# An encoder kernel on Trainium2: the attention's output projection moved behind the attention units and done in three rounded passes

## Chip, cores, metric

The kernel runs on one core of a Trainium2 chip. The metric is the device time of one execution in microseconds (us); the number quoted for a kernel is the median of its runs.

## What is computed

Two encoder layers work on 544 tokens: 512 rows of a prompt (4 tiles of 128) and 32 sample rows (tile 4). Layer 0 has a pooling mixer, layer 1 an attention with 16 heads of 64; both are followed by a mixture of 32 experts of which each token takes two. The part that matters here:

```python
o = band_attention(q, k, v, ...)           # softmax(q k^T / 8 + bias) v, per head, 64-row chunks
y = jnp.einsum('bse,ed->bsd', o, w_o)      # output projection, (rows x 1024) x (1024 x 1024)
x = x + y
h = rms_norm(x, norm_ffn[1])
x = x + hier_moe(h, ...)                   # router, then silu(h w_gate) * (h w_up) @ w_down per expert
```

The projection is float32. The kernel may compute it with float32 matmuls, or with operands split in a rounded part and a rest: `hi*hi + lo*hi + hi*lo` (`split_product`, used in both kernels for the QKV product).

## The kernel before, in words

Each engine has its own program; semaphores join them. TensorE (PE) does the matmuls, VectorE (DVE) and ScalarE (ACT) work on their results, SyncE (SP) issues nearly all loads of weights in a fixed order, GpSimd (POOL) loads the attention's biases and gathers token rows.

**Attention of layer 1.** The work is 36 units: 32 of the prompt (`unit(t)`: tile 3 first, then 2, 1, 0, with 8 pairs of heads each) and 4 of the sample rows. A unit of tile i has i + 1 blocks of 128 keys, so units 0 to 7 have four key blocks, 8 to 15 three, 16 to 23 two, 24 to 31 one. An iteration t of the loop holds, on PE, the scores of unit t (L2353), the transposes of unit t-2 (L2377) and the product with the values of unit t-3 (L2393; samples L2407, L2409). Between them DVE adds the bias (L1770), ACT takes the exponential (L1253), DVE scales (L1782), and the transposed weights go from PSUM to SBUF by ACT for the first head (L1264) and by DVE for the second (L1790). After every fourth unit ACT copies the four pairs' outputs into `oT` (L1277, `oT_out`). Each engine keeps its own program order, so an operation put between two others delays what stands behind it.

**Output projection.** `products_at(t)` puts 16 portions of four float32 matmuls (L2443, `tile_product`) behind the values of an iteration: every second iteration from t = 12 to t = 34, and then t = 35 to 38 for tile 0. A float32 matmul is two MATMUL instructions in the trace. Two portions make half a tile; DVE adds it to `x` (`add_product`, L1798). ACT then takes the squares of a row tile for the norm (`early_squares`, L1289), DVE scales the rows (L1349), and ACT stores them to `xn` in DRAM (`store_row`, L993), from where the experts' rows are gathered. The sample rows' product (`sample_product`, L2421) stacks four k-blocks in the four column strips of the array; ACT copies the result (`wo_stack_out`, L1283) and `sample_fold` (L2428) adds the four. `w_o` is loaded in 8 pieces of 512 KB into the buffers `pair`, which are gate 1 and up 1 of the experts.

**Loads.** Experts' gate, up and down weights (2 MB each) have three buffers each. Loads of the first experts of layer 1 are issued during the attention where their buffer is free: down 1, gate 0, down 2. Up 0 and down 0 follow once the attention's last output is copied, gate 1 and up 1 once the projection is done (`att_y`), gate 2 when the router's second logits are done, up 2 when all rows are stored and the first block gathered. Those for expert 3 wait for the products of expert 0, quarter by quarter (L665), and so on.

**Routing.** After the projection: transposes of `x` (L1864), logits (L1930, L1940), a long chain on DVE, then the first block's gather and the experts.

## Time and profile before

| | us |
|---|---|
| median of 3 runs | 1343.85 |
| lowest and highest | 1343.29, 1345.46 |
| span of the profiled execution, first to last instruction | 1340.0 |
| PE busy in it | 1291.8 |
| VectorE, ScalarE, GpSimd busy in it | 574.1, 304.7, 127.9 |
| mean granted TensorE clock | 0.986 of full speed |

The profile gives the profiled execution by its span; the median of the runs, which also holds what lies around the span, is 3.85 us above it. TensorE's busy time is modelled for overlapping matmuls, so where a sum needs the pace of matmuls it is taken from the distance between their starts.

### The profile page before, as it was taken

How to read it: one execution, taken by the hardware profiler on the slowest of the kernel's cores; microseconds unless marked ns; L12 is line 12 of the kernel's file. 1: busy time of each engine (PE TensorE's matmuls, PEld its weight loads, DVE VectorE, ACT ScalarE, POOL GpSimd, SP SyncE). 2: the span in 40 equal slices, each digit the busy share in tenths (PEclk: the TensorE clock that was granted, in tenths of full speed). 3: DMA queues.
4: the chain of work that ended last, by engine and by line, in shares of the span. 5: the costliest groups of instructions: out<-in, count | busy, mean ns of one | idle time of the engine just before them, and what ended most of it. 6: DMA issues, size and time to landing. Idle time of an engine off the chain costs nothing.

```text
span 1340.0 us, 19743 instructions
## 1 busy us (share of the span) xinstructions
PE 1291.8 (96%) x7448; PEld 638.2 (48%) x7448; DVE 574.1 (43%) x1062; ACT 304.7 (23%) x650; POOL 127.9 (10%) x205
## 2 busy tenths in 40 slices
PE   8899999999999999999999999899999999999998
PEld 6643344333343334788777544443444334343333
DVE  4543334433333433864419543543334334343433
ACT  4211111111111113443436432211111111111111
POOL 2010000000000000232233210000000000000000
PEclk9989999999999999999999999899999999999999
DMA  9989999999999999222058512999999999999996
GB/s 360 380 334 420 424 428 426 427 429 427 428 427 427 428 425 402 69 93 97 34 174 273 181 33 78 380 344 420 426 427 426 427 428 428 427 428 427 426 426 255
DMA packets 53569, 459.65 MB, mean 343 GB/s; under 512 B 8141, under 2 KB 9421, under 8 KB 28170
## 3 DMA queue, kind: packets, MB, share of 16 engines
q1 hardware_dynamic: 41246, 426.48, 76.5%
q0 software_dynamic: 9616, 23.95, 5.5%
q10 hardware_dynamic: 2652, 8.45, 1.7%
q8 instruction: 39, 0.64, 0.2%
q14 instruction: 16, 0.13, 0.0%
HBM read 455.44 MB, written 11.26 MB: 348 GB/s over the span
## 4 chain that ended last, share of the span: by engine, by line
PE 91%; issue 3%; DVE 3%; ACT 2%; DMA 1%; POOL 0%; SPq 0%; DVEq 0%; ACTq 0%; POOLq 0%
PE ps L2014 34%; PE ps L2045 11%; PE ps L2023 9%; PE ps L2024 8%; PE ps L2443 4%; PE ps L1843 3%; PE ps L1845 3%; PE ps L1844 3%; PE ps L2006 2%; PE ps L2377 1%; PE ps L2393 1%; PE ps L1916 1%; PE ps L2032 1%; PE ps L2353 1%; PE ps L1864 1%
## 5 line engine op out<-in xcount | busy, mean ns | idle before, releaser
L1592 DVE TENSOR_TENSOR x<-x,ps 128x1024 f32<-128x1024 f32 (+1 forms) x150 | 177.7, 1216 | 220.9 <-PE ps L2045 219.8
L1606 DVE SCALAR_TENSOR_TENSOR nat<-nat,slot_gate,ps 64x256 f32<-64x256 f32 x128 | 86.1, 672 | 196.3 <-ACT nat L1093 164.7
L2014 PE MATMUL ps<-pair,xT 128*64 128x512 f32 x352 | 163.8, 616 | 6.1 <-issue 6.1
L2014 PE MATMUL ps<-ring,xT 128*64 128x512 f32 x352 | 160.9, 606 | 8.0 <-issue 6.4
L2015 PE MATMUL ps<-pair,xT 128*64 128x512 f32 x352 | 164.0, 616 | 0.0
L2045 PE MATMUL ps<-y_parts,hot 64*128 64x512 f32 (+1 forms) x1200 | 161.3, 403 | 0.0
L2015 PE MATMUL ps<-ring,xT 128*64 128x512 f32 x352 | 161.1, 607 | 0.0
L2014 PE MATMUL ps<-third_pair,xT 128*64 128x512 f32 x320 | 143.6, 596 | 6.9 <-issue 6.9
L1093 ACT ACTIVATE nat<-ps 64x512 f32<-64x512 f32 x62 | 36.8, 594 | 485.5 <-PE ps L2015 485.5
L2024 PE MATMUL ps<-qk,hidT 128*64 128x512 f32 x320 | 144.9, 595 | 0.0
L2023 PE MATMUL ps<-qk,hidT 128*64 128x512 f32 x320 | 144.8, 595 | 0.0
L2015 PE MATMUL ps<-third_pair,xT 128*64 128x512 f32 x320 | 143.8, 597 | 0.0
L2045 PEld LDWEIGHTS ps<-y_parts,hot 64*128 64x128 f32 (+1 forms) x1200 | 98.9, 171 | 72.3 <-issue 48.7
L1569 DVE TENSOR_TENSOR y_parts<-ps,y_parts 128x512 fp32r<-128x512 f32 x60 | 41.5, 692 | 132.5 <-ACT y_parts L1078 132.5
L2014 PEld LDWEIGHTS ps<-pair,xT 128*64 128x64 f32 x352 | 46.9, 140 | 97.2 <-issue 96.0
L2014 PEld LDWEIGHTS ps<-ring,xT 128*64 128x64 f32 x352 | 46.3, 139 | 96.5 <-issue 95.5
L2014 PEld LDWEIGHTS ps<-third_pair,xT 128*64 128x64 f32 x320 | 41.4, 137 | 85.8 <-issue 84.7
L2023 PE MATMUL ps<-ring,hidT 128*64 128x512 f32 x176 | 79.6, 595 | 1.6 <-ACT xT L1059 1.6
L2024 PE MATMUL ps<-ring,hidT 128*64 128x512 f32 x176 | 79.7, 596 | 0.0
L1078 ACT ACTIVATE y_parts<-ps 128x512 fp32r<-128x512 f32 x60 | 35.8, 597 | 192.4 <-PE ps L2024 192.4
L1843 PE MATMUL ps<-w_hi,hT_hi 128*128 128x512 f32 x192 | 76.8, 400 | 0.7 <-DVE hT_lo L1374 0.7
L769 POOL DMA_INDIRECT nat<-xn,gcol x30 | 30.7, 1022 | 467.9 <-PE ps L2006 428.8
(261 smaller groups left out, 1780.3 us busy)
## 6 DMA issues: line engine op xcount, KB each, us to landing
qk<-in_moe_w_down SPq DMA_DIRECT2D x40, 2048.0 KB, 28.5
ring<-in_moe_w_down SPq DMA_DIRECT2D x22, 2048.0 KB
ring<-in_moe_w_gate SPq DMA_DIRECT2D x20, 2048.0 KB, 23.7
ring<-in_moe_w_up SPq DMA_DIRECT2D x20, 2048.0 KB
third_pair<-in_moe_w_gate SPq DMA_DIRECT2D x20, 2048.0 KB, 22.7
third_pair<-in_moe_w_up SPq DMA_DIRECT2D x20, 2048.0 KB
pair<-in_moe_w_gate SPq DMA_DIRECT2D x18, 2048.0 KB
pair<-in_moe_w_up SPq DMA_DIRECT2D x18, 2048.0 KB, 29.7
```

The lines of the kernel that those rows point to most:

```text
L1569: V.tensor_tensor(y_rest[v], ps[:, bank, :], f32(y_high[v]), ALU.subtract).then_inc(y_lo[l], 1)
L1592: return V.tensor_tensor(x[0:n, i, :], x[0:n, i, :], ps[0:n, bank:bank + 2, :].rearrange("p b c -> p (b c)"), ALU.add)
L1606: last = V.scalar_tensor_tensor(out=out[u * BLK:(u + 1) * BLK, :].rearrange("s (k p) -> s k p", k=n), in0=act_rows[:, u * n:(u + 1) * n, : ...
L1843: mm(out, x_hi, w_h, start=start, stop=False)
L1844: mm(out, x_lo, w_h, start=False, stop=False)
L1845: return mm(out, x_hi, w_l, start=False, stop=stop)
L2014: mm(ps[BLK:P, GU_BANK, :], rows, gate[:, at], start=(k == 0), stop=(k == KT - 1))
L2015: last = mm(ps[0:BLK, GU_BANK, :], rows, up[:, at], start=(k == 0), stop=(k == KT - 1))
L2023: mm(ps[0:BLK, bank, :], rows, slot[:, at:at + 512], start=(k == 0), stop=(k == FT - 1))
L2024: last = mm(ps[BLK:P, bank, :], rows, slot[:, at + 512:at + D], start=(k == 0), stop=(k == FT - 1))
L2045: last = mm(ps[0:n, bank + hf, :], (hot[v] if by is None else by)[slots, tok(i)], part[slots, :], start=first and at == 0, stop=final and ...
L2443: last = mm(ps[:, WO_BANK, :], oT[:, k, tok(i)], wo_all[:, k, hf * 512:(hf + 1) * 512], start=(k == 0), stop=(k == KT - 1))
```

## The change

The projection leaves the units. Iterations 0 to 39 hold only attention. The attention's outputs are copied to `oT_raw`, then rounded by ACT into `oT_hi` (`oT_rounded`), and DVE writes the rest into `oT_lo` (`oT_rest`), once for every four units. `w_o` comes in 16 pieces of 256 KB (piece c is half `c // 8`, k-block `c % 8`); ACT rounds each (`wo_rounded`) and DVE takes its rest (`wo_rest`). Pieces 0 to 3 are loaded and split among the units (t = 28 to 32); the others are loaded once the last unit's values are done (`o_ps`), the last four into places that the first half has used. Behind the units PE runs 16 pieces for 4 tiles in three passes, 192 matmuls of 128x512, and 32 more for the sample rows, whose two parts stand side by side in 64 columns instead of four k-blocks in four strips. Every half tile has a PSUM bank of its own.

From unit 16 on, ACT copies the transposed weights of both heads in one instruction, and DVE none. Gate 1 and up 1, whose buffers no longer hold `w_o`, are loaded at the start of the attention. Gate 0, whose buffer now holds pieces, comes in two parts: three quarters behind the first use of the pieces and the last quarter after the last tile's product. `early_squares` of tiles 3 to 1 come behind all pieces; their row scaling moves into the routing, before the logits' operations on DVE, and their stores behind the logits on ACT. The transposes of `x` wait for the norms of tiles 3 to 1.

```diff
+        WO_QUAD, WO_PARTS = 4, 2 * KT
+        wo_parts = [nc.alloc_sbuf_tensor_at("wo_ring", [P, 4, 2, 512], F32R, offset=ring_at),
+                    nc.alloc_sbuf_tensor_at("wo_nat", [P, NT, 2, 512], F32R, offset=nat_at),
+                    nc.alloc_sbuf_tensor_at("wo_gain", [P, 1, 2, 512], F32R, offset=gain_at),
+                    nc.alloc_sbuf_tensor_at("wo_xT", [P, 1, 2, 512], F32R, offset=xT_at)]
+        WO_PLACES = [(0, 0), (0, 1), (0, 2), (0, 3), (1, 0), (1, 1), (1, 2), (1, 3), (1, 4), (2, 0), (3, 0)]
+        WO_PLACE = list(range(11)) + [3, 4, 5, 6, 7]
...
+        WO_BANKS = ((5, 3, 1, 7), (7, 4, 2, 0))
+        WO_SAMPLE_BANKS = (6, 5)
...
+        WO_SPLIT = 28
+        WO_LOADS = [(0, range(0, 4)), (1, range(4, 8)), (2, range(8, 11)), (0, range(11, 12)), (1, range(12, 16))]
...
+        def group_at(t, behind):
+            g, at = divmod(t - behind, OT_GROUP)
+            return g if at == 0 and 0 <= g < GROUPS_OUT else None
...
+            def load_wo(c):
+                hf, k = divmod(c, KT)
+                sp.dma_start(wo_raw(c), wo[:, k, hf * 512:(hf + 1) * 512]).then_inc(piece_in[wo_landed(c)[0]], 16)
+            GATE_FIRST = 3 * QUART
             for l in range(L):
                 if l == 1:
+                    sp.wait_ge(s_ps, 2)
+                    load_gate(1, 1, 1)
+                    sp.wait_ge(s_ps, PAIRS)
+                    load_up(1, 1, 1)
                     sp.wait_ge(s_ps, LONG_UNITS)
                     load_down(1, 1, 1)
                     sp.wait_ge(pT_ps, 2 * LONG_UNITS)
-                    load_gate(1, 0, 0)
+                    for c in range(WO_QUAD):
+                        load_wo(c)
                     sp.wait_ge(s_ps, PROMPT_UNITS)
                     load_down(1, 2, 2)
-                    sp.wait_ge(oT_sb, OT_ALL)
+                    sp.wait_ge(v_out, 16 * NT)
+                    sp.wait_ge(v_second_out, 16 * NT)
+                    sp.wait_ge(o_ps, UNITS)
+                    for c in range(WO_QUAD, KT):
+                        load_wo(c)
+                    load_up(1, 0, 0)
+                    for c in range(KT, KT + 3):
+                        load_wo(c)
+                    load_down(1, 0, 0)
+                    sp.wait_ge(quarters_used, QKV_QUARTERS + 1)
+                    load_wo(KT + 3)
+                    sp.dma_start(gate_slots[0][:, 0:GATE_FIRST], weights(wg, NEXP)[:, 0:GATE_FIRST]).then_inc(parts_in, 16)
+                    sp.wait_ge(quarters_used, QKV_QUARTERS + 2)
+                    for c in range(KT + WO_QUAD, WO_PARTS):
+                        load_wo(c)
+                    sp.wait_ge(att_y, 2 * TILES)
+                    sp.dma_start(gate_slots[0][:, GATE_FIRST:], weights(wg, NEXP)[:, GATE_FIRST:]).then_inc(gate_in[0], 16)
                 else:
                     load_gate(0, 0, 0)
-                load_up(l, 0, 0)
-                load_down(l, 0, 0)
-                if l == 0:
+                    load_up(l, 0, 0)
+                    load_down(l, 0, 0)
                     load_gate(l, 1, 1)
                     load_up(l, 1, 1)
                     sp.wait_ge(x_mixed[0], NT)
                     load_down(l, 1, 1)
                     load_down(l, 2, 2)
-                else:
-                    sp.wait_ge(att_y, 2 * NT)
-                    load_gate(l, 1, 1)
-                    load_up(l, 1, 1)
...
+            def oT_rounded(g):
+                act.wait_ge(oT_sb, 2 * g + 1)
+                if g == GROUPS_OUT:
+                    act.activation(oT_sample[:, :, 0, :], oT_sample_raw, ACT.Copy).then_inc(oT_sb, 1)
+                else:
+                    at, cols = oT_columns(g)
+                    act.activation(oT_hi[:, at, cols], oT_raw[:, at, cols], ACT.Copy).then_inc(oT_sb, 1)
+            def wo_rounded(c):
+                s, count = wo_landed(c)
+                act.wait_ge(piece_in[s], count)
+                act.activation(wo_part(c, 1), wo_raw(c), ACT.Copy).then_inc(split_hi, 1)
...
             for t in range(UNITS + 4):
-                if t >= 4 and t - 4 < PROMPT_UNITS and (t - 4) % OT_GROUP == OT_GROUP - 1:
-                    oT_out(t - 4)
+                if group_at(t, OT_GROUP + 3) is not None:
+                    oT_out(group_at(t, OT_GROUP + 3))
                 if t < UNITS:
                     weights(t)
                 if t == FFN_GAIN_FREE:
                     act.dma_start(ffn_gain[:, :], A["norm_ffn"][1:2, :].broadcast_to((P, D))).then_inc(ffn_gain_in, 16)
                 if 0 <= t - 2 < UNITS:
                     pT_out(t - 2)
-                for i, hf in halves_before(t - 1):
-                    if hf == 1 and i > 0:
-                        early_squares(i)
+                if group_at(t, OT_GROUP + 4) is not None:
+                    oT_rounded(group_at(t, OT_GROUP + 4))
+                if 0 <= t - WO_SPLIT < WO_QUAD:
+                    wo_rounded(t - WO_SPLIT)
                 if t == UNITS:
                     load_sqrt_table()
-                    act.wait_ge(act_own, own[0])
-                    act.activation(std[:, 3, 1:TILES], ssq[:, 3, 1:TILES], ACT.Sqrt, bias=const("eps"),
-                                   scale=1.0 / D).then_inc(std_ready, TILES - 1)
-            oT_out(UNITS - 1)
+            oT_out(GROUPS_OUT)
+            oT_rounded(GROUPS_OUT)
+            for c in range(WO_QUAD, WO_PARTS):
+                wo_rounded(c)
             for i in range(TILES - 1, 0, -1):
-                store_row(1, i)
+                early_squares(i)
+            act.wait_ge(act_own, own[0])
+            act.activation(std[:, 3, 1:TILES], ssq[:, 3, 1:TILES], ACT.Sqrt, bias=const("eps"),
+                           scale=1.0 / D).then_inc(std_ready, TILES - 1)
...
+            for i in range(TILES - 1, 1, -1):
+                store_row(1, i)
             logitsT_out(1, 1)
+            store_row(1, 1)
...
+                    if l == 1:
+                        for i in ((TILES - 1, TILES - 2), (TILES - 3,))[part]:
+                            scaled_rows(3, i, route_row(i), ffn_gain)
...
+            def wo_rest(c):
+                dve.wait_ge(split_hi, QKV_QUARTERS + c + 1)
+                V.tensor_tensor(wo_part(c, 0), wo_raw(c), f32(wo_part(c, 1)),
+                                ALU.subtract).then_inc(split_lo, 1)
             for t in range(UNITS + 4):
-                for i, hf in halves_before(t):
-                    add_product(i, hf)
                 if t < UNITS:
                     biased(t)
                 if 0 <= t - 1 < UNITS:
                     scaled(t - 1)
-                if 0 <= t - 2 < PROMPT_UNITS:
+                if 0 <= t - 2 < LONG_UNITS:
                     pT_out(t - 2)
-                if t == UNITS + 1:
-                    dve.wait_ge(std_ready, 3 * NT + TILES - 1)
-                    dve.wait_ge(ffn_gain_in, 32)
-                    link(V.reciprocal(rstd[:, 3, 1:TILES], std[:, 3, 1:TILES]))
-                if t > UNITS:
-                    i = TILES - 1 - (t - UNITS - 1)
-                    scaled_rows(3, i, route_row(i), ffn_gain)
+                if group_at(t, OT_GROUP + 5) is not None:
+                    oT_rest(group_at(t, OT_GROUP + 5))
+                if 0 <= t - WO_SPLIT - 1 < WO_QUAD:
+                    wo_rest(t - WO_SPLIT - 1)
+            oT_rest(GROUPS_OUT)
+            for c in range(WO_QUAD, KT + WO_QUAD):
+                wo_rest(c)
+            for i in range(TILES - 1, -1, -1):
+                add_product(i, 0)
+            for c in range(KT + WO_QUAD, WO_PARTS):
+                wo_rest(c)
+            for i in range(TILES - 1, -1, -1):
+                add_product(i, 1)
+            dve.wait_ge(std_ready, 3 * NT + TILES - 1)
+            dve.wait_ge(ffn_gain_in, 32)
+            link(V.reciprocal(rstd[:, 3, 1:TILES], std[:, 3, 1:TILES]))
...
+            def part_product(hf, i, k):
+                c = hf * KT + k
+                pe.wait_ge(split_lo, QKV_QUARTERS + c + 1)
+                return split_product(ps[:, WO_BANKS[hf][i], :], oT_hi[:, k, tok(i)], oT_lo[:, k, tok(i)],
+                                     wo_part(c, 1), wo_part(c, 0), k == 0, k == KT - 1)
+            def sample_product(hf, k):
+                c = hf * KT + k
+                pe.wait_ge(split_lo, QKV_QUARTERS + c + 1)
+                out = ps[:, WO_SAMPLE_BANKS[hf], :]
+                both = oT_sample[:, k, :, :].rearrange("p u t -> p (u t)")
+                if k == 0:
+                    mm(out[0:2 * SS, :], both, wo_part(c, 1), start=True, stop=False)
+                    return mm(out[0:SS, :], oT_sample[:, k, 0, :], wo_part(c, 0), start=False, stop=False)
+                mm(out[0:SS, :], oT_sample[:, k, 0, :], wo_part(c, 0), start=False, stop=False)
+                return mm(out[0:2 * SS, :], both, wo_part(c, 1), start=False, stop=(k == KT - 1))
...
             pe.wait_ge(kcT_sb, 2)
             for t in range(UNITS + 4):
                 if t < UNITS:
                     scores(t)
                 if t in (1, 2):
-                    keep_busy(1, WO_BANK, ident, some)
+                    keep_busy(1, SPARE_WO_BANK, ident, some)
                 if 0 <= t - 2 < UNITS:
                     p_transposes(t - 2)
                 if 0 <= t - 3 < UNITS:
                     values(t - 3)
-                if products_at(t) is not None:
-                    tile_product(*products_at(t))
+            pe.wait_ge(oT_lo_sb, GROUPS_OUT * (TILES - 1) // TILES)
+            for k in range(WO_QUAD):
+                for i in range(TILES - 1, 0, -1):
+                    part_product(0, i, k)
+            pe.wait_ge(oT_lo_sb, GROUPS_OUT)
+            for k in range(WO_QUAD):
+                part_product(0, 0, k)
+            pe.wait_ge(oT_lo_sb, GROUPS_OUT + 1)
+            for k in range(WO_QUAD):
+                last = sample_product(0, k)
+            last.then_inc(quarters_used, 1)
+            for k in range(WO_QUAD, KT):
+                for i in range(TILES - 1, -1, -1):
+                    last = part_product(0, i, k)
+                    if k == KT - 1:
+                        last.then_inc(att_y, 1)
+                last = sample_product(0, k)
+            last.then_inc(quarters_used, 1)
+            for k in range(KT):
+                for i in (TILES - 1, TILES - 2):
+                    last = part_product(1, i, k)
+                    if k == KT - 1:
+                        last.then_inc(att_y, 1)
+            for i in range(TILES - 3, -1, -1):
+                if i == 0:
+                    pe.wait_ge(x_half, TILES)
+                    for k in range(KT):
+                        last = sample_product(1, k)
+                    last.then_inc(stack_ps, 1)
+                for k in range(KT):
+                    last = part_product(1, i, k)
+                last.then_inc(att_y, 1)
+            pe.wait_ge(std_ready, 3 * NT + TILES - 1)
             transposes(3, TILES - 1)
-            for hf in range(2):
-                sample_product(hf)
```

TensorE, among the units with one key block (L2353 and L2468 scores, L2377 and L2492 transposes, L2393 and L2508 values, L2443 a portion of the projection). Before:

```order
L2353 MATMUL ps<-qk 128x128 x2
L2377 MATMUL ps<-cst,ring 128x128 x2
L2393 MATMUL ps<-ring,nat 64x128 x2
L2353 MATMUL ps<-qk 128x128 x2
L2377 MATMUL ps<-cst,ring 128x128 x2
L2393 MATMUL ps<-ring,nat 64x128 x2
L2443 MATMUL ps<-pair,third_pair 128x512 x4
L2353 MATMUL ps<-qk 128x128 x2
L2377 MATMUL ps<-cst,gain 128x128 x2
L2393 MATMUL ps<-ring,nat 64x128 x2
```

Now:

```order
L2468 MATMUL ps<-qk 128x128 x2
L2492 MATMUL ps<-cst,ring 128x128 x2
L2508 MATMUL ps<-ring,nat 64x128 x2
L2468 MATMUL ps<-qk 128x128 x2
L2492 MATMUL ps<-cst,ring 128x128 x2
L2508 MATMUL ps<-ring,nat 64x128 x2
L2468 MATMUL ps<-qk 128x128 x2
L2492 MATMUL ps<-cst,gain 128x128 x2
L2508 MATMUL ps<-ring,nat 64x128 x2
```

The portion behind every second iteration is gone; the attention's instructions are the same.

TensorE, at the end of the last units (L2407, L2409, L2522, L2524 values of the samples; L1864 the transposes of `x`). Before:

```order
L2409 MATMUL ps<-ring,nat 64x32 x2
L2443 MATMUL ps<-pair,third_pair 128x512 x4
L2407 MATMUL ps<-ring 64x32 x2
L2409 MATMUL ps<-ring,nat 64x32 x2
L2407 MATMUL ps<-ring 64x32 x2
L2409 MATMUL ps<-ring,nat 64x32 x2
L2443 MATMUL ps<-pair,third_pair 128x512 x4
L1864 MATMUL ps<-cst,x 128x128 x8
L2421 MATMUL ps<-pair,third_pair 32x512 x16
L1864 MATMUL ps<-cst,x 128x128 x8
```

Now (L1956 to L1958 are the three passes of `split_product`):

```order
L2524 MATMUL ps<-ring,nat 64x32 x2
L2522 MATMUL ps<-ring 64x32 x2
L2524 MATMUL ps<-ring,nat 64x32 x2
L2522 MATMUL ps<-ring 64x32 x2
L2524 MATMUL ps<-ring,nat 64x32 x2
L2522 MATMUL ps<-ring 64x32 x2
L2524 MATMUL ps<-ring,nat 64x32 x2
L1956 MATMUL ps<-wo_ring,oT_hi 128x512
L1957 MATMUL ps<-wo_ring,oT_lo 128x512
L1958 MATMUL ps<-wo_ring,oT_hi 128x512
L1956 MATMUL ps<-wo_ring,oT_hi 128x512
```

What stood between the samples' values is now one run of 224 matmuls behind them, and the transposes of `x` follow that run.

ScalarE, units 29 to 31 (L1253 and L1307 exponentials, L1264 and L1321 copies of transposed weights, L1277 and L1337 copies of outputs, L1353 the rounding of a piece). Before:

```order
L1264 ACTIVATE ring<-ps 128x128
L1253 ACTIVATE ring<-ring 128x128 x2
L1264 ACTIVATE ring<-ps 128x128
L1277 ACTIVATE third_pair<-ps 128x4x128
L1253 ACTIVATE gain,ring<-gain,ring 128x128 x2
L1264 ACTIVATE ring<-ps 128x128
L1253 ACTIVATE ring<-ring 128x160
```

Now:

```order
L1321 ACTIVATE ring<-ps 128x2x128
L1353 ACTIVATE wo_ring<-ring 128x512
L1307 ACTIVATE ring<-ring 128x128 x2
L1321 ACTIVATE ring<-ps 128x2x128
L1353 ACTIVATE wo_ring<-ring 128x512
L1337 ACTIVATE third_pair<-ps 128x4x128
L1307 ACTIVATE gain,ring<-gain,ring 128x128 x2
L1321 ACTIVATE ring<-ps 128x2x128
L1353 ACTIVATE wo_ring<-ring 128x512
```

A rounding of a piece stands behind each copy, and the copy takes both heads.

## Rows read from the trace of the kernel before

**Rows 1.** The page: span, and GB/s of the DMA engines in 40 slices of 33.5 us.

```profile
span 1340.0 us, 19743 instructions
...
GB/s 360 380 334 420 424 428 426 427 429 427 428 427 427 428 425 402 69 93 97 34 174 273 181 33 78 380 344 420 426 427 426 427 428 428 427 428 427 426 426 255
```

**Rows 2.** Window of 20 us: busy of PE, PEld, DVE, ACT, POOL; clock, DMA share, GB/s.

```profile
860.00:880.00 20.00, 17.82 (x65) 8.18 (x66) 17.26 (x63) 2.55 (x5) 1.98 (x2) 0.85 0.77 296
```

**Rows 3.** Timeline of SyncE's DMA queue: start, length, line, target and source.

```profile
858.63 0.33 SPq L617 DMA_DIRECT2D third_pair<-in_moe_w_gate  x1
...
877.02 0.33 SPq L665 DMA_DIRECT2D ring<-in_moe_w_gate  x1
```

**Rows 4.** Chain that ended last: start, length, engine, tile, line.

```profile
731.41 0.85 PE ps L2353 x8
...
736.53 3.63 PE ps L2443 x8
...
822.51 3.63 PE ps L2443 x8
...
827.30 3.63 PE ps L2443 x8
...
840.30 0.89 PE ps L1864 x8
```

**Rows 5.** Instruction groups, 704 to 841 us: shapes, count, busy us, mean ns.

```profile
L2443 PE MATMUL ps<-pair,third_pair 128*128 128x512 f32 x128 | 59.2, 605 | 0.0
...
L1277 ACT ACTIVATE third_pair<-ps 128x512 f32<-128x512 f32 x8 | 4.6, 579 | 0.0
```

**Rows 6.** Timeline of a one-key-tile unit: start, length, engine, line.

```profile
801.69 0.49 PE L2353 MATMUL ps<-qk 64*128 64x128 f32 x4
...
802.66 0.40 ACT L1253 ACTIVATE ring<-ring 128x128 f32<-128x128 f32 x1 [3.14 <-DVE ring L1770]
...
803.44 0.25 ACT L1264 ACTIVATE ring<-ps 128x128 f32<-128x128 f32 x1
...
803.75 0.44 PE L2377 MATMUL ps<-cst,ring 128*128 128x128 f32 x2 [0.41 <-ACT ring L1264]
...
804.49 0.70 PE L2443 MATMUL ps<-pair,third_pair 128*128 128x512 f32 x1
```

**Rows 7.** Timeline of a two-key-tile unit.

```profile
757.64 0.70 PE L2353 MATMUL ps<-qk 64*128 64x256 f32 x4
...
758.95 0.51 ACT L1253 ACTIVATE ring<-ring 128x256 f32<-128x256 f32 x1 [4.79 <-DVE ring L1770]
...
760.58 0.63 PE L2377 MATMUL ps<-cst,ring 128*128 128x128 f32 x4
```

**Rows 8.** DVE group in the QKV product, 543 to 700 us.

```profile
L1361 DVE TENSOR_TENSOR w_lo<-ring,w_hi 128x1024 fp32r<-128x1024 f32 x20 | 31.0, 1563 | 46.3 <-ACT w_hi L940 46.2
```

**Rows 9.** Timeline of ScalarE among the last units.

```profile
827.87 1.28 ACT L960 ACT_TABLE_LOAD   x1
```

**Rows 10.** Timeline of TensorE in the QKV product.

```profile
542.82 0.39 PE L1843 MATMUL ps<-w_hi,hT_hi 128*128 128x512 f32 x1
...
545.77 0.39 PE L1844 MATMUL ps<-w_hi,hT_lo 128*128 128x512 f32 x1
```

**Rows 11.** Timeline of TensorE and ScalarE behind the last tile product.

```profile
841.17 3.64 PE L2421 MATMUL ps<-pair,third_pair 128*32 128x512 f32 x32
...
844.49 1.06 ACT L1283 ACTIVATE gain<-ps 128x512 f32<-128x512 f32 x2
...
847.66 1.50 PE L1864 MATMUL ps<-cst,x 128*128 128x128 f32 x11
```

**Rows 12.** DMA issues, 690 to 900 us: count, KB each, median us to landing.

```profile
xn<-third_pair ACTq DMA_DIRECT2D x4, 512.0 KB, 10.8
...
ring<-in_rel_bias_reversed POOLq DMA_DIRECT2D x5, 256.0 KB, 6.1
```

**Rows 13.** Window of 1 us in the routing; columns as in the second group.

```profile
856.00:857.00 1.00, 1.00 (x8) 0.87 (x9) 0.54 (x2) 0.00 (x0) 0.00 (x0) 0.50 0.96 410
```

150 lines of the change are left out of this document (76 added, 74 removed).

## The prediction

> **What bounds the kernel now.** I read the page first, then the windows of the routing, SyncE's queue, the chain of waits, and last the timelines of single units. The page's GB/s line has two plateaus near 427, one for each layer's experts, and a valley between them, the attention [rows 1]. Two facts follow. Once the second plateau is reached the experts are paced by their weights, so whatever the change gains or loses before it shifts the end by as much. And the plateau doesn't begin when a weight happens to be ready early: in the routing the DMA engines already have slack, 0.77 busy over 20 us [rows 2], and expert 3's first quarter is issued only at 877.02, when expert 0 has used its buffer [rows 3]. Before expert 0 starts, all free buffers are full in both kernels. So gate 1 and up 1 during the attention save nothing by themselves: they only restore what moving `w_o` out of their buffers and behind the units would otherwise delay.
>
> What is left is the path from iteration 12 of the units to the routing. In the chain it is nearly all TensorE: iterations and portions of the projection in turn, each portion 3.63 us, from the first at 736.53 to the transposes of `x` at 840.30 [rows 4], 103.8 us. The 64 float32 matmuls are 128 instructions in that stretch [rows 5]; 16 portions x 3.63 = 58.1 us. The other 45.7 us are iterations 13 to 39. They are so short because each portion hides the latency of a unit: the other engines finish their step while TensorE multiplies.
>
> **Term 1, the units without portions: +7.1 us.** I rebuild iterations 13 to 39.
> - Three key blocks: 731.41 to 736.53 is two iterations without a portion, 2.56 each [rows 4]. Three of them (13 to 15) take 7.7. Iterations 16 to 18 mix three and two blocks; at about 2.35 they take 7.1.
> - Two key blocks: the loop goes through two iterations. Scores' start to exponential's start is 1.31, from there to the transposes 1.63, and the transposes and values take about 0.60 each [rows 7]: 4.14, with the larger copy of both heads 4.2, so 2.1 each. Five iterations: 10.5.
> - One key block: 801.69 to 804.49 is two iterations, 2.80 [rows 6]; the exponentials hold ScalarE 0.78 (802.66 to 803.44), the copy is now twice as long, so 1.45 to 1.5 each. Iterations 26 and 27: 3.0. Iterations 24 and 25, with two-block transposes, about 1.8 each: 3.6.
> - Iterations 28 to 32 carry the pieces. ScalarE has 0.78 + 0.35 + a rounding of 0.55 (priced as the copy of 512 columns, 0.579, less its overlap [rows 5]) = 1.7, and 2.3 where a group's copy or rounding joins. VectorE has two biases, the scaling and a subtraction of half the size of the one in the QKV product, 1.563 / 2 = 0.78 [rows 8], so also about 1.9 to 2.3. I take 2.3, 2.3, 1.8, 2.3, 1.6: 10.3.
> - Samples, 33 to 35: TensorE's own small matmuls, 1.5 + 1.4 + 2.0 = 4.9. Iterations 36 to 38: 827.30 - 822.51 - 3.63 = 1.16 each [rows 4], 3.5. The last copy stands behind a group's rounding (0.55) and the table load of 1.28 [rows 9], of which TensorE covers some 0.5: +1.3, so 4.8.
> - The copy of a group's output, which the next values wait for, was hidden by a portion; I give these waits 1.0.
>
> The sum is 7.7 + 7.1 + 10.5 + 3.0 + 3.6 + 10.3 + 4.9 + 4.8 + 1.0 = 52.9 against 45.7, rounded +7.1. Bounds: +1 if only TensorE's work counted, +13 if each wait is exposed in full.
>
> **Term 2, the portions go: -58.1 us**, as above.
>
> **Term 3, the run of rounded products: +50.8 us.** The QKV product has the same form of three passes; 542.82 to 545.77 is 13 intervals, 0.227 us each [rows 10]. 64 products x 3 = 192, and the samples' 32 (two for each of 16 pieces): 224 x 0.227 = 50.8. The samples alone cost 7.3, where four strips at once took 3.64 [rows 11]. Cover for the pieces: 4 to 7 are loaded when the last values end, while 56 matmuls (12.7 us) on pieces 0 to 3 run. The last four wait for the first half and are wanted 24 matmuls, 5.4 us, later. A 256 KB load that shares the engines with a 2 MB load takes 6.1 us [rows 12], with 0.6 + 0.8 for rounding and rest 7.5; that would expose 2.1. By then no other load is left in the queue, so I take 0 and keep +2.1 as the bound.
>
> **Term 4, behind the run: -1.9 us.** From the end of the last portion, 840.30, to the next pair of transposes at 847.66 were 7.4 us, of which the samples' product took 3.64 [rows 4, 11]. It has moved into term 3. But the fold still waits for ScalarE's stacked copies, which started at 844.49 behind the squares of tile 0 [rows 11]; these need the last product just as before. So only about half of 3.64 comes out; bounds 0 and -3.6.
>
> **Costs taken at nothing.** Row scaling of tiles 3 to 1 in the routing, 3 x about 1.2 us of VectorE, stands ahead of logits for which VectorE waited; if that cover were too small, up to 1 us. The stores of these rows: tile 1's is now issued just behind the load of gate 2, issued at 858.63 [rows 3]. A store under load took 10.8 us [rows 12], which ends near 870, when the first gather is about to start; 0, bound +3. Gate 1 and up 1 share the engines with the first biases, as the eight pieces of `w_o` did before: 0, bound +1.
>
> **Sum.** +7.1 - 58.1 + 50.8 - 1.9 = -2.1 us: the profiled span goes from 1340.0 to 1337.9, and the median, 3.85 above the span before, from 1343.85 to **1341.8**. Two kernels of this length can be told apart at about 0.2%, 2.7 us, so this is within what counts as no change, by little.
>
> **One rule against the change.** Where TensorE has short, sparse work, its granted clock is at the lower level, 0.50 of full speed (1.2 GHz) in the window at 856 [rows 13], and 0.85 on average over 860 to 880, that is 6 of 20 us at half [rows 2]. In the units it never fell, and each pair of them contained a portion of dense work. The Trainium skill (TensorE: Matmul & The Clock Gate, section "HAM oscillation") says that bursts of matmuls with idle time between them make the clock fall again each time, so that the next burst starts slow. By that rule the units with one key block, which now leave TensorE idle a quarter to a half of the time, would run at the lower level, and so would the first stretch of the product; the sum would be that of the first rival.
>
> **The rivals.**
> - *Slower: the clock falls in the short units.* At half speed the scores, transposes and values of one block (0.42 + 0.37 + 0.37 = 1.16 by the starts in [rows 6]) add 1.16 to two iterations, 0.58 each, to 15 iterations at most 8.7; with half of it hidden or at the full clock, 4.3. The product's first stretch at half clock, as long as the 6 us of [rows 2], costs 3. Together +7: 1349. For: iterations 28 to 35 are paced by the others. Against: TensorE is still busy over half of each iteration, and the clock stayed up among the three-block units without portions. It decides from +4.8 us on. Chance 0.22.
> - *Faster: the latencies hide after all.* If ScalarE and VectorE keep up, term 1 is +1.5 and the time is 1336.2. For: two iterations in [rows 6] took 2.80 including a wait of 0.41, so the loops are not far above TensorE's own work. Against: that pair started with everything ready. Chance 0.16.
> - *Faster: bytes.* If the end is set by bytes alone, 4 MB loaded earlier at 427 GB/s are 9.8 us: 1332. Against: the buffers, as said. Chance 0.04.
> - *Late pieces or stores.* +3: 1345. Chance 0.10.
>
> **How the numbers follow.** My forecast has 0.48, with its own range 1338.5 to 1345. Below 1341.15 (faster) lie nearly half of it, 0.20, and both faster rivals: 0.40. Within 2.7 us of 1343.85 lie the rest of it and most of the late pieces: 0.35. Slower is the clock's case and a remainder: 0.25. The range 1335 to 1350 holds the two large rivals and leaves out the bytes and the far ends of the bounds.
>
> **What would show it.** Right: iterations of two blocks near 2.1 us and of one block near 1.5, about 2 with pieces; last values near 789; 224 matmuls in 50.8 us without a wait; transposes of `x` near 840; the first quarter of expert 3 some 2 us earlier than 877. A clock of 0.5 between 765 and 800 shows the first rival, a gap in the middle of the run late pieces, a first gather that waits for stores the late stores. The forecast is wrong if the last values end before 785 or after 794, or if expert 3's first quarter moves by another amount than the end of the kernel.

## The result, and the profile after

The changed kernel takes 1348.66 us, the median of 13 executions, beside 1343.29 us for the kernel before on the same chip. The ratio is 1.0037, with a 95% interval of 1.0028 to 1.0047: +5.0 us, slower by more than the 0.2% that can be told apart. Taken again later (e15 below) it was 1.0032 (1.0016 to 1.0048). The forecast of 1341.8 was wrong, and the time is that of the first rival, 1349; it lies within the range of 1335 to 1350.

The profiled execution took 1347.7 us with a span of 1345.9, so 1.8 us lie around the span. By the same 1.8 the profiled execution of the kernel before took 1341.8. Between the two spans are 5.9 us, of which 2.3 were there before anything changed: the first unit's scores start at 699.92 in the one and at 702.22 in the other. Over all profiled executions below, of kernels whose programs are equal up to there, this start lay between 698.0 and 707.5, so it differs from execution to execution. It goes with the clock as well. The changed kernel's profile has 6.8 us at half clock from 15.4 on, the one before has none there (the window from 14 to 24, first of the kernel before and then of the changed one; the clock is the third number from the end). In e13, the latest start, 10.2 us are at half clock from 14.4 on, and 3.4 each near 485 and 564:

```profile
14.00:24.00 10.00, 9.02 (x66) 8.51 (x66) 5.96 (x8) 5.13 (x10) 7.12 (x8) 1.00 1.05 382
14.00:24.00 10.00, 10.00 (x48) 9.02 (x47) 5.77 (x8) 5.13 (x10) 7.38 (x9) 0.66 1.04 389
```

What is left to explain in the profile is +3.6 us, against the -2.1 forecast: 5.7 us.

The page of the changed kernel, by the side of [rows 1]. The second plateau of GB/s begins in the slice in which it began before (the 28th, 419 and 420):

```profile
span 1345.9 us, 19904 instructions
...
PEclk8989999999999999999999979889999999999999
DMA  9889999999999999222057663489999999999996
GB/s 363 350 333 420 426 426 427 427 427 427 429 427 429 426 425 402 71 91 96 34 182 254 184 227 124 145 316 419 427 426 428 427 427 426 429 428 427 427 425 258
```

New in the clock's line are the 7, the slice from 774 to 807, and the 8 of the first slice, which has a 9 in the kernel before. Windows of the last units, the samples and the first product matmuls (start:end, length, busy of PE, PEld, DVE, ACT, POOL, clock, DMA share, GB/s):

```profile
770.00:774.00 4.00, 3.42 (x32) 1.95 (x28) 2.51 (x17) 3.66 (x15) 2.21 (x6) 1.00 0.39 74
774.00:778.00 4.00, 2.58 (x22) 1.40 (x20) 3.73 (x17) 3.86 (x14) 0.78 (x2) 1.00 0.61 136
778.00:782.00 4.00, 2.70 (x41) 1.72 (x42) 3.07 (x14) 3.54 (x12) 0.20 (x1) 0.74 0.98 296
782.00:786.00 4.00, 4.00 (x56) 2.47 (x48) 2.02 (x9) 2.11 (x8) 0.00 (x0) 0.50 0.65 270
...
794.00:798.00 4.00, 4.00 (x12) 3.14 (x12) 0.42 (x1) 0.58 (x2) 0.00 (x0) 0.62 0.72 231
798.00:802.00 4.00, 4.00 (x20) 3.28 (x19) 2.12 (x4) 2.19 (x4) 0.00 (x0) 1.00 1.06 424
```

TensorE is busy 2.58 and 2.70 of 4 us from 774 to 782, with ScalarE at 3.86 of 4 in the first of them, and its clock falls at 780.0 to 0.50 of full speed (1.2 GHz). It comes back at 797, in the run of products. From 782 on TensorE itself bounds the samples, busy 4.00 of 4. In the kernel before the clock was 1.00 over all of this stretch:

```profile
774.00:778.00 4.00, 3.57 (x30) 2.23 (x29) 3.60 (x16) 3.02 (x11) 1.64 (x3) 1.00 0.19 31
```

The timeline of TensorE at the start of the run shows the matmuls at both levels, 0.43 us from start to start and then 0.22 to 0.24:

```profile
793.66 0.80 PE L1956 MATMUL ps<-wo_ring,oT_hi 128*128 128x512 f32 x1
794.26 0.63 PE L1957 MATMUL ps<-wo_ring,oT_lo 128*128 128x512 f32 x1
794.68 0.63 PE L1958 MATMUL ps<-wo_ring,oT_hi 128*128 128x512 f32 x1
...
797.16 0.40 PE L1958 MATMUL ps<-wo_ring,oT_hi 128*128 128x512 f32 x1
797.40 0.39 PE L1956 MATMUL ps<-wo_ring,oT_hi 128*128 128x512 f32 x1
```

Ahead of all this, from 714 to 775, the chain of waits of the changed kernel goes twelve times through a load of a unit's bias, 3.35 to 10.17 us each; in the kernel before it does so once (3.54 us at 782.77). Two of the twelve:

```profile
768.27 3.35 DMA gain<-in_rel_bias_reversed
771.91 3.36 DMA ring<-in_rel_bias_reversed
```

In the middle of the run the last four pieces are late. They are issued at 821.12, rounded from 826.67, their rests follow from 827.33, and TensorE, whose matmul before them started at 826.17, goes on at 828.08, 1.7 us late:

```profile
821.12 1.75 SPq L664 DMA_DIRECT2D nat<-in_attn_w_o  x4
...
826.67 2.19 ACT L1353 ACTIVATE wo_nat<-nat 128x512 fp32r<-128x512 f32 x4 [12.33 <-DMA nat<-in_attn_w_o]
827.33 2.50 DVE L1904 TENSOR_TENSOR wo_nat<-nat,wo_nat 128x512 fp32r<-128x512 f32 x4 [5.97 <-ACT wo_nat L1353]
...
828.08 0.50 PE L1956 MATMUL ps<-wo_nat,oT_hi 128*128 128x512 f32 x1 [1.52 <-DVE wo_nat L1904]
```

Behind the run, the chain of waits of the changed kernel (start, length, engine, tile, line), the counterpart of [rows 4, 11]:

```profile
848.43 0.89 PE ps L1977 x8
...
881.02 0.61 PE ps L2127
```

From 848.43 to expert 0's first matmul at 881.02 are 32.6 us, where the kernel before took 34.75 (840.30 to 875.05). Expert 3's first quarter is issued at 882.99, 5.97 later than in [rows 3], and the end is 5.9 later: what happens ahead of the experts comes out at the end one for one.

### The profile page after: what moved, and what is told of

Its sections match the earlier page's. It is cut to its first block, busy times and chain, and to the rows that moved or that the text cites. A ratio compares the mean times of both kernels' runs of the same rounds, so it can differ in the third digit from the quotient of the medians.

```text
span 1345.9 us, 19904 instructions
## 1 busy us (share of the span) xinstructions
PE 1288.9 (96%) x7512; PEld 659.4 (49%) x7512; DVE 585.6 (44%) x1071; ACT 321.3 (24%) x675; POOL 128.3 (10%) x205
## 4 chain that ended last, share of the span: by engine, by line
PE 88%; DMA 5%; issue 3%; DVE 3%; ACT 2%; SPq 0%; POOL 0%; DVEq 0%; ACTq 0%; POOLq 0%
PE ps L2127 33%; PE ps L2158 11%; PE ps L2136 9%; PE ps L2137 8%; PE ps L1956 4%; PE ps L1958 4%; PE ps L1957 4%; DMA ring<-in_rel_bias_reversed 2%; PE ps L2119 2%; PE ps L2029 1%; PE ps L2145 1%; DMA ffn_gain<-in_rel_bias_reversed 1%; PE ps L2367 1%; PE ps L1977 1%; DMA gain<-in_rel_bias_reversed 1%
## 5 line engine op out<-in xcount | busy, mean ns | idle before, releaser
L2127 PE MATMUL ps<-pair,xT 128*64 128x512 f32 x352 | 160.8, 607 | 5.9 <-issue 5.9
L2128 PE MATMUL ps<-pair,xT 128*64 128x512 f32 x352 | 160.9, 607 | 0.0
L1956 PE MATMUL ps<-w_hi,hT_hi 128*128 128x512 f32 x192 | 76.8, 400 | 0.7 <-DVE hT_lo L1459 0.7
```

Source lines behind the costliest of these rows:

```text
L1956: mm(out, x_hi, w_h, start=start, stop=False)
L2127: mm(ps[BLK:P, GU_BANK, :], rows, gate[:, at], start=(k == 0), stop=(k == KT - 1))
L2128: last = mm(ps[0:BLK, GU_BANK, :], rows, up[:, at], start=(k == 0), stop=(k == KT - 1))
```

## The experiments

My theory was now the first rival's: the clock. Its rivals were the late pieces, the loads of gate 1 and up 1 among the units, and the stores and loads behind the run. Fifteen kernels went to the chip in four sets, and each set shares some 29 executions of the kernel before. "Ratio" is to the kernel before, with its 95% interval; the clock is TensorE's mean over each span, averaged over all executions of a kernel. The kernel before stands at 0.986 in each set. e4 and e8 have 6 executions, e9 has 7, the others 12 or 13. The clock in the last column is that of the whole span and does not say where in it the clock was low.

| kernel | median us | ratio | mean clock |
|---|---|---|---|
| the change | 1348.66 | 1.0037 (1.0028 to 1.0047) | 0.979 |
| e1 wide dummies | 1349.35 | 1.0038 (1.0021 to 1.0055) | 0.983 |
| e2 three tiles | 1346.61 | 1.0024 (1.0011 to 1.0036) | 0.979 |
| e3 33 matmuls among the samples | 1347.62 | 1.0031 (1.0015 to 1.0046) | 0.984 |
| e4 gate 1, up 1 behind the run | 1350.80 | 1.0053 (1.0033 to 1.0073) | 0.977 |
| e5 gate 2 behind the stores | 1346.35 | 1.0039 (1.0020 to 1.0057) | 0.979 |
| e6 18 early matmuls, three tiles | 1342.62 | 0.9994 (0.9981 to 1.0008) | 0.982 |
| e7 = e6 and e5 | 1340.68 | 0.9985 (0.9970 to 1.0000) | 0.983 |
| e8 gate 1, up 1 behind the stores | 1351.70 | 1.0063 (1.0041 to 1.0084) | 0.978 |
| e9 kernel before with e5's edit | 1347.64 | 1.0044 (1.0021 to 1.0066) | 0.984 |
| e10 = e7, 21 early, from step 26 | 1339.26 | 0.9986 (0.9969 to 1.0003) | 0.984 |
| e11 18 dummies, three tiles | 1346.47 | 1.0029 (1.0015 to 1.0044) | 0.982 |
| e12 = e7 again | 1342.02 | 0.9986 (0.9968 to 1.0004) | 0.983 |
| e13 one thin dummy a step, three tiles | 1344.26 | 1.0007 (0.9989 to 1.0025) | 0.982 |
| e14 two thin dummies a step | 1346.02 | 1.0011 (0.9996 to 1.0026) | 0.984 |
| e15 the change again | 1347.27 | 1.0032 (1.0016 to 1.0048) | 0.979 |

### e1: dummies of full width

```diff
+                if 24 <= t < UNITS:
+                    w = 512 if t < PROMPT_UNITS else 256
+                    mm(ps[:, SPARE_WO_BANK, 0:w], ident, some[:, 0:w], start=True, stop=True, skip_group_check=True)
```

> The changed kernel with one dummy matmul a unit behind the scores of units 24 to 35 on TensorE (128x512 f32, 0.59 us at the full clock, for units 24 to 31; half as wide for 32 to 35), into the bank that stands idle there; everything else as in the change. The changed kernel stands at 1.0037 of the kernel before (+5.0 us). Theory A (the granted clock of 0.50 between 780 and 797 costs the sample units and the first product matmuls their time): the clock stays at 1.00 through 770 to 800, the first seven product matmuls take 0.227 us each in place of about 0.43 (-1.6), the sample units come every 1.5 instead of 2.0 us (-2 to -3), the dummies lie in TensorE's waits; the kernel gets 3 to 4.5 us faster than the change, +0.5 to +2 against the kernel before. Rival B (the units are paced by ScalarE and VectorE or by the bias loads, and the clock only follows): the last values end where they did, 793.7, or later by what of the 12 dummies (6 us) isn't hidden; -1.6 at best, up to 3 us slower.

A miss by the time: 1.0038, the change's own. In its profile the clock held through the last units and most of the samples (it fell at about 791), but the dummies of 0.59 us pushed the units back: the scores of unit 24 start at 763.4 and the last prompt unit's at 779.0, 15.6 us later; in the change from 764.8 to 776.6, 11.8 us. In the profile, then, what the clock gave the samples was largely paid by the dummies, and the end of the clock's fall still hit the run (0.50 from 794 to 798). The experiment tells neither way.

### e2: three tiles on pieces 8 to 11

```diff
             for k in range(KT):
-                for i in (TILES - 1, TILES - 2):
+                for i in (TILES - 1, TILES - 2, TILES - 3) if k < WO_QUAD else (TILES - 1, TILES - 2):
                     last = part_product(1, i, k)
...
-                for k in range(KT):
+                for k in range(WO_QUAD if i == TILES - 3 else 0, KT):
                     last = part_product(1, i, k)
```

> The changed kernel with pieces 8 to 11 of the output weights multiplied for three tiles (3, 2, 1) before piece 12 is asked for, not for two: 36 rounded matmuls (8.2 us at 0.227) stand between the last use of pieces 4 to 7 and the first of piece 12, in place of 24 (5.4). Nothing else moves. Theory A (pieces 12 to 15 are late: loads issued at 821.12 land in 4.2 us, rounding and rest take until 828.08, TensorE stands about 1.9 us and the piece-paced start a little more): the gap closes wholly, 1.5 to 2.5 us faster than the change. Rival B (the time behind the run is set by the row scaling and the stores or by the first expert's weights, so that an earlier end of the run is given back): the run ends 2 us earlier, but the time is that of the change within 0.5 us.

The gap is gone from the trace, the run has no wait left, and the ratio falls from 1.0037 to 1.0024, about 1.7 us (the intervals overlap). That is theory A, and the size of the gap itself. The run still took 53.7 us, because in this execution the clock stayed at 0.50 until about 798.

### e3: 33 matmuls among the last units and samples

```diff
+            EARLY = {30: [(3, 0)], 31: [(3, 1)], 32: [(3, 2)], 33: [(3, 3)], 34: [(2, 0), (2, 1)],
+                     35: [(2, 2), (2, 3)], 36: [(1, 0)], 37: [(1, 1), (1, 2)], 38: [(1, 3)]}
...
                     values(t - 3)
+                for i, k in EARLY.get(t, ()):
+                    pe.wait_ge(oT_lo_sb, (TILES - i) * PAIRS // OT_GROUP)
+                    part_product(0, i, k)
-            for k in range(WO_QUAD):
-                for i in range(TILES - 1, 0, -1):
-                    part_product(0, i, k)
```

> The changed kernel with 33 of the 36 rounded matmuls of pieces 0 to 3 for tiles 3, 2 and 1 put among the last units and samples (three or six behind the values of each step, from unit 30 on) and not all behind them; the banks are those of the change. Theory A (TensorE has idle time in the short units and samples, and real matmuls there take work out of the run and keep the clock up): 33 times 0.227 = 7.5 us leave the run, the last values end 3 to 5 us later than at the full clock, about where they did at 793.7; the clock may still fall at 780, since the first of them comes at 777; 3 to 6 us faster than the change. Rival B (TensorE is the bound of the samples, at half clock 2.0 of 2.04 us a unit busy, so that a matmul put there only moves): the last values end 7.5 to 10 us later and the time is that of the change within 1 us.

The clock never fell from 766 to 806. 7.5 us of matmuls were added and the last values ended only 3.1 us later than in the change (796.8 for 793.7). But the ratio was only 0.0006 better, 0.8 us, and the profile shows both places where the gain went. First, pieces 4 to 7 can be loaded only when the last values have read `v_nat`, and now too little work covered them. In the timelines of TensorE and VectorE of this kernel:

```profile
805.34 0.50 PE L1956 MATMUL ps<-wo_nat,oT_hi 128*128 128x512 f32 x1 [3.06 <-DVE wo_nat L1904]
...
804.59 1.90 DVE L1904 TENSOR_TENSOR wo_nat<-nat,wo_nat 128x512 fp32r<-128x512 f32 x3 [6.43 <-ACT wo_nat L1353]
```

Second, the chain behind the run goes through the last row's store:

```profile
864.98 11.10 DMA xn<-third_pair
...
876.94 2.75 DMA nat<-xn,gcol_first
```

### e4: gate 1 and up 1 behind the products

```diff
-                    sp.wait_ge(s_ps, 2)
-                    load_gate(1, 1, 1)
-                    sp.wait_ge(s_ps, PAIRS)
-                    load_up(1, 1, 1)
...
+                    sp.wait_ge(att_y, 2 * NT)
+                    load_gate(1, 1, 1)
+                    load_up(1, 1, 1)
```

> The changed kernel with the loads of gate 1 and up 1 (2 MB each) taken out of the attention and put behind the products, where the kernel before has them. Theory A (these 4 MB hold back the bias loads of units 3 to 12, whose landing took 7.3 us once): the waits of GpSimd on the biases before unit 12 shrink, unit 12's scores start up to 1 us earlier; the time falls by 0 to 1 us. Rival B (they cost nothing there, and save bandwidth behind the run, where gate 2, up 2 and expert 0's quarters are loaded): the same within 0.5 us, or 0.5 to 2 us slower if the loads behind the run collide with the gathers and the first expert's weights.

Slower by 2 us, as the third part of rival B says, and its profile shows the price of the clock into the bargain. The units before 775 differ little: from the first scores to those of the last prompt unit are 73.9 us, and 74.3 in the change. So the loads in the attention cost the units 0.4 us, although GpSimd waited 7.4 us for one bias there. But from the last prompt unit's scores to the last values' end are 13.4 us (775.5 to 788.9) where the change took 17.2 (776.56 to 793.73): here the clock was 1.00 until 786.2, although TensorE was busy only 2.13 of 4 us from 774 to 778.

```profile
774.00:778.00 4.00, 2.13 (x20) 1.22 (x24) 3.93 (x18) 4.00 (x16) 0.40 (x2) 1.00 0.84 208
778.00:782.00 4.00, 3.64 (x67) 2.25 (x68) 3.53 (x16) 3.38 (x12) 0.00 (x0) 1.00 0.95 385
782.00:786.00 4.00, 3.81 (x62) 2.65 (x60) 1.65 (x8) 3.17 (x13) 0.00 (x0) 1.00 0.21 86
786.00:790.00 4.00, 3.58 (x33) 2.89 (x32) 0.43 (x2) 2.16 (x6) 0.00 (x0) 0.53 0.01 4
```

I read these 3.8 us as what the half clock costs the samples; it is the difference of one profile of each of two kernels. All of it is lost again behind the run, where 4 MB issued at 850.15 and gate 2 at 860.96 run beside the last store, 14.71 us in the chain:

```profile
861.65 14.71 DMA xn<-third_pair
```

### e5: gate 2 waits for the row stores

```diff
                 sp.wait_ge(logitsT_ps, 2 * (l + 1))
+                if l == 1:
+                    sp.wait_ge(xn_stored[l], 16 * NT)
                 load_gate(l, 2, 2)
```

> The changed kernel with one edit on the queue of loads: gate 2 of the second layer (2 MB, issued at 864.57 in the changed kernel, just as the last row store is issued) waits until the stores of the normalised rows have landed. Theory A (the rest of the loss behind the products is the stores sharing the DMA engines with gate 2: where the chain of waits goes through the last store it takes 11.1 us, in the run with gate 1 and up 1 there as well 14.7): the last store lands some 5 us earlier, the gather of the first expert's rows goes when VectorE's row numbers are there (about 874 on the changed kernel's clock, for 876.2), expert 0 starts 1 to 2 us earlier, the time falls by 1 to 2 us. Rival B (the row numbers of VectorE and GpSimd's own start set the gather, not the store): the same within 0.5 us, or slower by up to 1 if gate 2 comes late.

Not decided: the ratio is that of the change (1.0039), with a wide interval. In its profile expert 0 starts 31.4 us behind the run, where the change took 32.6. In the change's own profiled execution the first gather waited for VectorE's row numbers, not for a store; in the profile of the change taken again (e15) it did wait for the store, which was issued 0.7 us behind gate 2 and took 10.57 us. So the collision is there in some executions of the same kernel and not in others.

### e6 and e7: 18 early matmuls, and gate 2 behind the stores

```diff
+            EARLY = {30: [(3, 0)], 31: [(3, 1)], 33: [(3, 2)], 35: [(3, 3)], 37: [(2, 0)], 38: [(2, 1)]}
...
+                for i, k in EARLY.get(t, ()):
+                    pe.wait_ge(oT_lo_sb, (TILES - i) * PAIRS // OT_GROUP)
+                    part_product(0, i, k)
...
                 for i in range(TILES - 1, 0, -1):
-                    part_product(0, i, k)
+                    if (i, k) not in sum(EARLY.values(), []):
+                        part_product(0, i, k)
```

That is e6, with e2's edit; e7 has e5's as well.

> The changed kernel with 18 rounded matmuls (pieces 0 to 3 of tile 3, pieces 0 and 1 of tile 2) spread three by three over the steps 30, 31, 33, 35, 37, 38 of the units, and pieces 8 to 11 multiplied for three tiles before piece 12. 38 matmuls (8.8 us at 0.23) are left to cover the 8.5 us from the last values to piece 4, where the run with 33 early ones stood 3.1 us. Theory A (the loss is the clock that falls, 4 us in the samples and 1.6 to 1.9 in the first product matmuls, and the late pieces, 1.5 to 3): the clock stays at 1.00 through 800, no gap over 0.5 us in the run, the last values end 1.5 to 3 us before the changed kernel's (samples at full clock -4, early matmuls +1 to +2.5), the run takes 206 times 0.23 = 47.5 us; the products end 6 to 9 us earlier than in the change; with the start of the first expert following by three quarters or more, the time falls by 5 to 8 us, to 1 to 3 us below the kernel before. Rival B (what is gained at the products' end is given back behind it, to stores and loads, as in the run with 33 early ones, where 2 of 3.4 us were): the products end as said, but the time falls by 2 to 4 us.

> Both edits of the two kernels before this one in one: 18 matmuls among the last units and samples, three tiles on pieces 8 to 11, and gate 2 behind the row stores. Theory A (clock, late pieces and the collision of stores and gate 2 are three separate costs): its time is that of the kernel with 18 early matmuls less 2 us or more, since the more the products end early the more the store is the last; 7 to 10 us below the change, 2 to 5 below the kernel before. Rival B (the store isn't what is late): the same as with 18 early matmuls alone, within 0.7 us.

e6 is 4.0 us faster than e2 by medians and no longer to be told from the kernel before. Its profile keeps the clock at 1.00 through the samples and has no gap; the last values end 89.8 us behind the first scores (the change 91.5), the run from there takes 47.8 us (the change 54.6). Together that is 8.5 us. 1.7 of them are given back behind the run, where the chain now goes through a store of 10.60 us, so that 6.8 reach the end of the profile; by ratio it is 5.8 against the change. The mean clock, 0.977 to 0.986 over the executions, leaves room for a fall among the units in some of them. e7 takes another 1.9 us off by medians (1.2 by ratio, and the intervals overlap), with the chain now past the stores. These are windows of e7, to be set beside the change's:

```profile
774.00:778.00 4.00, 3.48 (x22) 2.09 (x22) 3.07 (x17) 3.32 (x12) 0.20 (x1) 1.00 0.93 215
778.00:782.00 4.00, 3.77 (x57) 2.27 (x59) 3.37 (x13) 3.05 (x11) 0.00 (x0) 1.00 0.93 385
...
794.00:798.00 4.00, 4.00 (x20) 3.25 (x18) 0.24 (x1) 0.91 (x2) 0.00 (x0) 1.00 0.93 336
```

### e8 and e9: the same wait elsewhere

```diff
                 sp.wait_ge(logitsT_ps, 2 * (l + 1))
+                if l == 1:
+                    sp.wait_ge(xn_stored[l], 16 * NT)
+                    load_gate(1, 1, 1)
+                    load_up(1, 1, 1)
                 load_gate(l, 2, 2)
```

This is e8, with e4's loads taken out of the attention. e9 is the kernel before with e5's two lines.

> The changed kernel with gate 1 and up 1 out of the attention, loaded behind the row stores and before gate 2, which waits for the stores too. The run with these two loads right behind the products was 2 us slower than the change: its products ended 4.2 us earlier (start of the units taken out), but the last store took 14.7 us. Theory A (the loads in the attention cost the units nothing, the 4 us were the clock, which fell 6 us later there by chance; the loss was the store): the units run as in the change, with the clock falling somewhere between 778 and 790, the last store takes 5 to 6 us, and the time is that of the run with stores first, within 1 us. Rival B (the 4 MB in the attention do hold the units up by 4 us): the last values end again at 789 to 790, and with the store free the time is 4 us or more below the change.

> The kernel before with the one edit of the stores: gate 2 of the second layer waits until the normalised rows have landed; nothing of the change. It tells what of the 2 us between the kernels with 18 early matmuls without and with this edit belongs to the change. Theory A (the collision of the last row store with gate 2 is in the kernel before as well, its stores took 10.8 us and it stood 34.75 us behind the products): 1 to 2.5 us faster than the kernel before. Rival B (in the kernel before the store isn't what ends last, since expert 0's weights and the rows leave the queue in another order): the same within 0.5 us; then the whole 2 us are won from the change's shape.

Both are misses on the time and agree with each other. e8's units run as e4's to 0.1 us, and its clock falls at 786.3, e4's at 786.2, where in the four profiles with these loads in the attention and no matmuls added (the change, e2, e5, e15) it falls at 772 to 780. So the later fall isn't mere chance of one execution, though what sets it stays open; and rival B's "4 us or more below" doesn't come, since the loads now meet the gather. In e8 it took 8.58 us and in e9 5.75, where it took 2.75 to 3.07 in the other chains that pass it. e8's chain:

```profile
872.51 8.58 DMA nat<-xn,gcol_first
```

and e9's:

```profile
871.91 5.75 DMA nat<-xn,gcol_first
```

Behind the stores comes the gather, and a 2 MB load put off from the one lands on the other. In the kernel before the chain doesn't pass the stores, though they took 10.8 us [rows 12], so there the wait only costs. In the profiles expert 0 starts 36.9 us behind the products for 34.9, and from there to the end another 1.3 us are lost: 3.3 of the 5.9 us that the ratio of 1.0044 makes. With 7 executions, the rest stays open. What e5's edit gains in e7 belongs to that kernel's order of things.

### e10 and e12: pieces rounded earlier, and e7 once more

```diff
-        WO_SPLIT = 28
+        WO_SPLIT = 24
...
+            EARLY = {26: [(3, 0)], 28: [(3, 1)], 29: [(3, 2)], 31: [(3, 3)], 33: [(2, 0)], 35: [(2, 1)], 37: [(2, 2)]}
```

> The kernel with 18 early matmuls and stores first, but pieces 0 to 3 are rounded four units earlier (from unit 24 on, not 28), and 21 matmuls stand among the units from step 26 on in place of 18 from step 30. 35 matmuls and more (8.1 us) are left for the 8.5 us to piece 4. Over all its executions the kernel with 18 had a mean clock of 0.983 (0.977 to 0.987), the kernel before 0.986, the change 0.979. Theory A (the clock still falls in some executions because TensorE idles before its first early matmul at about 775): the mean clock over the executions rises to 0.985 or more and the time falls by another 1 to 2 us. Rival B (TensorE is by no means idle in the two-block units, and ScalarE and VectorE bound the short ones, into which the roundings move): no more than 0.5 us either way, or 0.5 to 1.5 us slower, from the two-block units with 1.4 us more of rounding work.

> The kernel with 18 early matmuls, three tiles and stores first once more, on the chip of the other three, so that it stands beside them and beside the kernel before a second time. It stood at 0.9985 [0.997, 1.0000]. Theory A (its gain is real): 0.9975 to 0.9990 again, 7 us below the change. Rival B (the first set of executions was a lucky one for the clock): 0.9995 to 1.0010.

e7's gain repeats (0.9986), on another chip. e10 gives the same ratio, with a median 2.8 us lower than e12's and 3.9 below the kernel before, but with an upper interval that reaches 1.0003: rival B within what can be told. The clock rose only from 0.983 to 0.984.

e12's profile is worth more than its ratio. It is the same program as e7, both profiled executions start their units at 700.3, and up to unit 30 they agree to within 1 us (its scores start at 772.64 in e7 and at 772.20 in e12). Then e12's clock falls, from 774.6 to 781.4 and again from 791.6 to 798.4, where e7's stays at 1.00. e12:

```profile
774.00:778.00 4.00, 3.89 (x19) 2.12 (x17) 2.91 (x16) 2.87 (x11) 0.20 (x1) 0.57 0.74 182
778.00:782.00 4.00, 4.00 (x44) 2.47 (x42) 2.09 (x8) 2.05 (x8) 0.00 (x0) 0.58 0.89 332
...
794.00:798.00 4.00, 4.00 (x11) 3.13 (x10) 0.00 (x0) 0.00 (x0) 0.00 (x0) 0.50 1.01 341
```

Neither has a wait in its run. e12's run ends at 843.04 and e7's at 838.17, 4.9 us apart, and the spans are 1340.9 and 1336.4. So within one program 13.7 us at half clock in this stretch went with 4.9 us more. It also shows that 18 matmuls among the units don't hold the clock in every execution.
Three sets of executions of this shape stand about 1.9 us below the kernel before in ratio, each with an interval that just reaches 1; against the change, 6 to 7 us less by ratio, they are clear.

### e11, e13, e14: activity alone

e11 has the places of e6 but three dummies at each, and the whole run behind; e13 and e14 have one or two dummies where TensorE waits for ScalarE's copy. All have e2's edit; e13 and e14 also round pieces 0 to 3 from unit 24 on. This is e13; e14 has `range(2)`.

```diff
+                if t == 27:
+                    pe.wait_ge(split_lo, QKV_QUARTERS + 1)
+                    pe.wait_ge(oT_lo_sb, 1)
+                if 27 <= t < 40:
+                    for _ in range(1):
+                        mm(ps[:, SPARE_WO_BANK, :], oT_hi[:, 0, tok(TILES - 1)], wo_part(0, 1), start=True, stop=True)
```

> The kernel with three tiles on pieces 8 to 11, plus 18 rounded dummy matmuls at the places where the kernel with 18 early ones has real ones (steps 30, 31, 33, 35, 37, 38), of the same operands, into the idle bank; the run behind the units is whole, all 224 matmuls. So no work leaves the run, and only TensorE's activity among the units is added. The kernel with three tiles had a mean clock of 0.979 over its executions and stood at 1.0024 of the kernel before, the one with 18 real early matmuls 0.982 and 0.9994. Theory A (the clock is the larger part of the change's loss, 4 us in the samples and 1.9 behind them, and activity alone brings it back): the clock keeps up through the samples, the last values end 1.5 to 3 us before those of the kernel with three tiles, the run loses its 1.9 us of half clock: 3 to 4.5 us faster in an execution in which the clock holds, 1.5 to 3.5 us faster by medians. Rival B (the 4 us between those two kernels are the 18 matmuls that left the run, 4.1 us, and the clock is worth little): the same as the kernel with three tiles within 1 us, or up to 2 us slower from the 4.1 us of added matmuls.

> The kernel with three tiles on pieces 8 to 11, plus one rounded dummy matmul (128x512, 0.23 us) behind the scores of each step from 27 to 39, where TensorE waits some 0.6 us for ScalarE's copy; pieces 0 to 3 are rounded from unit 24 on. No matmul leaves the run. Theory A (the clock alone is worth 3 to 5 us where it holds): the clock at 780 to 790 stays at 1.00 in the profiled execution, the mean clock over the executions rises from 0.979 to 0.982 or more, 2 to 4 us faster than the change repeated beside it by medians beyond the 1.5 of the three tiles (so 3.5 to 5.5 in all). Rival B (the gain of the kernels with early matmuls is the work that left the run): 1 to 2 us faster than the change, that of the three tiles, whatever the clock. Rival C (a third of a microsecond a step is too little to hold it): the clock falls as before and the time is B's.

> The same with two dummy matmuls a step (26, 6.0 us in all, of which some 0.45 us a step in TensorE's waits). Theory A: the clock holds more surely than with one (mean over the executions 0.983 or more), and costs little where TensorE waits but up to 0.2 us a step in the samples: 2 to 5 us faster than the change. Rival B: the time of the three tiles or up to 2 us slower than that.

> The changed kernel as it is, beside the two with dummies. All theories: 1.0030 to 1.0045 of the kernel before, mean clock over the executions 0.978 to 0.980 where the kernel before has 0.986; in the profiled execution the clock falls somewhere between 774 and 790 and comes back at 796 to 800.

e11 held the clock in its profiled execution and was 3.4 us faster in it than e2 (span 1341.1 for 1344.5, with the first scores at 700.3 and 700.6), but not by medians: over its executions the clock was 0.979 to 0.986, and the 4.1 us of dummies are there in each of them. e13 and e14 put less in. With one thin dummy a step and no work taken out of the run, e13 is at 1.0007, where the change beside it is at 1.0032: 3.0 us by medians (1344.26 for 1347.27), of which 1.7 are e2's. So activity alone, less what the dummies cost, is worth 1 to 2 us by medians. Over e13's twelve, the four with a clock of 0.980 or less took 1346.9 to 1350.5 us, the eight above it 1341.8 to 1346.2. But this is the clock of the whole span: e13's profiled execution is one of the four, and of its 59.7 us at half clock only 10.2 lie near the samples (792.7 to 802.9), while 30.7 lie ahead of the units, whose scores start at 707.45, 5 us later than the change's. That is less than theory A's 2 to 4, and more than rival B's none; the difference of 1.3 us over B is at the edge of what the intervals bear. e14 is at 1.0011, 1.3 us below e15 by medians and 2.8 by ratio; below theory A's 2 to 5 by the one and within it by the other. It holds the clock in its profiled execution from 774 to the end of the run, but behind the run the chain goes through a store of 11.00 us and 4 us are lost against the change's profile:

```profile
782.00:786.00 4.00, 4.00 (x57) 2.59 (x55) 2.46 (x14) 2.90 (x11) 0.00 (x0) 1.00 0.70 295
786.00:790.00 4.00, 4.00 (x52) 2.94 (x48) 1.13 (x3) 2.58 (x6) 0.00 (x0) 1.00 0.01 2
790.00:794.00 4.00, 4.00 (x35) 3.06 (x36) 0.42 (x1) 1.32 (x5) 0.00 (x0) 1.00 0.17 45
```

Its run of 224 matmuls at the full clock without a gap took 51.1 us (792.52 to 843.59): 0.228 each. e15's profile shows the change itself with another pattern, the clock at 0.50 from 772.0 to 778.8 and from 785.7 to 792.5, earlier at both ends than I had expected, and the same wait of 1.5 us for the late pieces.

## Why the prediction was wrong

**By its own steps.** In the profile the terms came out so:

| step | predicted | measured |
|---|---|---|
| start of the units | 0 | +2.3, from execution to execution |
| term 1, units without portions | +7.1 | +9.2 |
| term 2, the portions | -58.1 | -58.1 |
| term 3, the run | +50.8 | +54.7 |
| term 4, behind the run | -1.9 | -2.2 |
| sum without the start | -2.1 | +3.6 |

The iterations themselves came out as forecast until the clock fell. Two key blocks took 2.24 us each (2.1), one block 1.56 (1.5), those with pieces 1.98 (about 2); from the scores of unit 13 to those of unit 33 it was 42.6 us for 42.2. The samples behind them took 12.3 us for 9.7 and the 1.0 of waits; in e4 they took 9.7. (52.9 less 45.7 is +7.2; I wrote +7.1.) What the forecast did not have is the loads of the biases in the chain. As the sum of these units still fits, nothing here shows that they cost time, and no run made them faster to see.

**The step that failed** is the sentence on the clock: I put the forecast's 0.48 on a clock that stays up, because TensorE "is still busy over half of each iteration". It was: 2.58 of 4 us at 774 to 778. The clock fell nevertheless at 780.0, and two terms of the sum came out too low by it. What makes it fall is not settled by the busy share: e4 kept it for 8 us more behind a window with 2.13 of 4, and of the one program of e7 and e12 it stayed in e7 behind a window of 2.71 (770 to 774) and fell in e12 behind one of 2.78. The two terms:
- The samples: 17.2 us at half clock, 13.4 in e4, whose clock was full for all but the last 2.7 of them; 3.8 us. Without them term 1 would be +5.4, below the +7.1; my latencies were on the dear side, and within the bounds.
- The first product matmuls: eight intervals in 3.50 us where 8 x 0.227 = 1.82 are due, 1.7 us. With the gap of 1.7 and e14's 51.1 for a clean run that makes 54.5 of the 54.7. The term itself, 50.8, was right to 0.3.

**How far the clock carries the whole +5.0.** The profile has 17 us more at half clock than the kernel before (56.0 for 39.1), as much as the stretch from 780 to 797. The other stretches at 0.50 are equal in sum but not in place: the change has the 6.8 us near 15 that go with its later start, the kernel before has 3.4 near 422 and 3.4 near 1224 that the change lacks. Over all executions the mean clock was 0.979 against 0.986, and 0.0069 x 2 x 1345 = 18.6 us more at half clock, so the profiled execution is no exception. Between executions of one kernel, here 88 of the kernel before, 0.001 less clock goes with 0.74 us more time (correlation -0.74); 6.9 such steps are 5.1 us. That is a relation and not a proof, since other disturbances can move both, and the stretches can lie anywhere in the span. By the experiments: the clock's share in the profile is 3.8 + 1.7 = 5.5 us. The pair e7 and e12, one program, gives 4.9 us for 13.7 us at half clock, by which the change's 17.1 would be worth about 6.1 (an estimate from that pair). Dummies bring back some 1.3 of it by medians, at a cost of their own and only in part of the executions. Real matmuls at the same places, together with what they take out of the run, bring back 4.0 (e6 against e2). How the 4.0 divide into clock and hidden work by medians wasn't settled.

**Late pieces.** I took 0 for the wait with +2.1 as its bound, arguing that no other load is left in the queue. It was 1.7, and e2 got it back. The load took 5.6 us from its issue to the rounding (821.12 to 826.67), with nothing beside it, and only the cover of 24 matmuls, 5.4 us, had been counted right. Rounding and rest, 1.4 us, had to come on top; the load could have been hidden only if it took 4.0.

**The start behind the run.** Term 4 was right, -2.2 for -1.9. The stores at nothing, bound +3, were too sure: in the change's first profile the chain passes them by, in e15's and six others' it goes through a store of 10.6 to 11.4 us, and with the loads behind them (e4) through one of 14.7. Gate 1 and up 1 in the attention, at nothing with bound +1, cost 0.4 us there (e4) and save 2 us behind the run; the forecast's sentence that they "only restore" what moving `w_o` would otherwise delay is borne out.

**The first rival** named place, mechanism and size: 1349 for 1348.66, clock of 0.5 between 765 and 800. Its working was less good than its sum, and that the sum was hit to 0.3 us is luck. The units with one key block hardly ran at the lower level; the samples behind them did, and the product's first stretch cost 1.7 rather than 3. Its +7 met 5.5 us of clock and 1.7 of late pieces, which were another rival's. By the Trainium skill (TensorE: Matmul & The Clock Gate, section "HAM oscillation") matmuls in bursts, with waits between them, let the clock fall again, and the next burst starts slow. The trace agrees in what came of it, with matmuls of 0.43 us at the start of the run. It differs in what went before: the section's example has long waits for DMA between its bursts, and here TensorE's longest pause from 768 to 780 was 0.84 us, with 2.58 of 4 us busy. Its chance of 0.22 was too low: the same rule stood against the change in writing, and the only evidence I had against it were three-block units, which keep TensorE far busier (4.96 of 5.12 us from 731.41 to 736.53 in the kernel before).

## What to carry to other kernels

When filler work is moved out of a latency-bound stage, ask what TensorE's activity in that stage will be without it, and price both the stage and the first microseconds of the dense work behind it at half clock; a clock that held in the fuller version is no evidence. A small part of the work may be enough: 18 of 224 matmuls left among the last units and two repairs behind them turned a loss of 0.37% into a gain of about 0.15%, with intervals that just reach none; enough work must stay behind to cover the loads that start there. And a load that is put off from one transfer lands on the next, so look at the whole sequence of store, gather and weights on the queue before moving it.

## What was unexpected of the hardware

- The clock isn't the same from one execution to the next of one kernel: the mean over the span lay between 0.974 and 0.982 for the change taken again, with times of 1345.4 to 1354.1 us, and the stretch at half clock began at 780 in one profile and at 772 in another. A stretch of 6.8 to 10.2 us at half clock near 15 us stood in three profiles (the change, e9, e13), whose units start at 702.2, 702.4 and 707.5; in the eight profiles with no stretch at half clock ahead of the units but those near 64, 85, 361 and, in most, 422, they start at 699.9 to 700.7.
- One gather of the first expert's rows takes 2.75 to 3.07 us where no 2 MB load was issued in the 5.5 us before it, 5.75 with a 2 MB load issued 3.6 us before it, and 8.58 with three, issued 4.9 to 5.8 us before it.
- A row store of 512 KB issued 0.1 to 0.7 us behind a 2 MB load took 10.6 to 11.4 us in seven profiles, and 14.7 with two more such loads in the queue. Without such a load beside them the stores' median was 4.7 to 5.1 us (e5, e7, e8, e12).
